# Two attention stages of a two-block transformer: values matmuls of three steps issued together

## The reference, cut to what matters

```python
# stick_breaking_attention, per head
z = einsum('bqhd,bshd->bhqs', q_blk, k) * scale
log_1m = where(causal, log_sigmoid(-z), 0.0)
excl = cumsum(log_1m, axis=3, reverse=True) - log_1m
a = where(causal, exp(log_sigmoid(z) + excl), 0.0)
o = einsum('bhqs,bshd->bqhd', a, v)
# nsa_attention, per kind ("selected" and "window"), per head
s = where(valid, einsum(q_rot, k) * scale, NEG)
o_kind = einsum(softmax(s), v)           # p @ v, twice, plus a compressed branch
out = einsum('bsch,bschd->bshd', gates, [o_cmp, o_sel, o_win]) @ w_o
```

## Time and profile before

| | us |
|---|---|
| median of 3 runs | 2097.75 |
| the profiled execution | 2098.55 |
| its span, first to last instruction | 2096.8 |
| steps of the stick-breaking heads that have an output matmul in them | 902.7 to 1046.9 of the span |
| steps of the NSA heads from the second pair of kinds on | 1571.8 to 1699.5 of the span |

### The profile page before, as it was taken

The page is one execution under the profiler, slowest core; times in us unless marked ns, Lnnn a source line. Parts: engine busy times, 40 slices in busy tenths (PEclk is TensorE's granted clock), DMA queues, the critical chain, the costliest instruction groups (busy, mean ns, idle before and its releaser), DMA issues.

```text
span 2096.8 us, 31979 instructions
## 1 busy us (share of the span) xinstructions
PE 2078.5 (99%) x12566; PEld 1749.0 (83%) x12566; DVE 1520.8 (73%) x2061; ACT 989.0 (47%) x1655; POOL 717.2 (34%) x588
## 2 busy tenths in 40 slices
PE   9999999999999999999999999999999999999998
PEld 6888688888999998777689999988975678899997
DVE  6866775658988886387768787766578757777774
ACT  4433564445544454355554333344537755334344
POOL 2301520027443434054463232301147646323221
PEclk9999999999999999999999999999999999999999
DMA  6233135223323333211133323233520022332321
GB/s 181 91 107 85 51 101 171 71 71 101 106 86 106 116 96 96 81 51 52 40 91 101 121 81 121 83 119 91 152 75 2 1 60 82 101 113 88 115 87 51
DMA packets 293303, 188.44 MB, mean 90 GB/s; under 512 B 9249, under 2 KB 287009, under 8 KB 293153
## 3 DMA queue, kind: packets, MB, share of 16 engines
q1 hardware_dynamic: 292864, 186.18, 29.7%
q10 hardware_dynamic: 288, 0.21, 0.1%
HBM read 183.48 MB, written 2.10 MB: 89 GB/s over the span
## 4 chain that ended last, share of the span: by engine, by line
PE 92%; DVE 4%; ACT 2%; issue 1%; DMA 0%; POOL 0%; ACTq 0%; SPq 0%; DVEq 0%
PE ps L542 90%; PE ps L576 2%; DVE wl L515 1%; ACT wh L505 1%; DVE sb_small L3478 0%; DMA p_xt<-in_x 0%; DVE ns_x L3524 0%; DVE ns_x L3523 0%; DVE tp_up L2330 0%; DVE H L679 0%; DVE nt_pts L3506 0%; DVE st_L L2735 0%; ACT XH L563 0%; DVE tp_up L675 0%; DVE tt_t L2071 0%
## 5 line engine op out<-in xcount | busy, mean ns | idle before, releaser
L515 DVE TENSOR_TENSOR wl<-raw,wh 128x1024 fp32r<-128x1024 f32 (+1 forms) x334 | 429.3, 1299 | 240.5 <-ACT wh L505 239.8
L542 PE MATMUL ps<-xb_x,wh 128*128 128x256 f32 (+1 forms) x1584 | 388.4, 336 | 1.4 <-DVE st_k L2780 0.6
L505 ACT CAST wh<-raw 128x1024 fp32r<-128x1024 f32 (+1 forms) x334 | 322.5, 981 | 132.1 <-PE ps L542 119.9
L542 PEld LDWEIGHTS ps<-xb_x,wh 128*128 128x128 f32 x1584 | 265.6, 188 | 31.1 <-DVE H L679 0.9
L542 PE MATMUL ps<-tt_t,wh 128*128 128x256 f32 x1536 | 277.4, 280 | 0.8 <-ACT tp_q L2257 0.3
L542 PE MATMUL ps<-xb_x,wl 128*128 128x256 f32 (+1 forms) x792 | 264.5, 334 | 0.0
L542 PEld LDWEIGHTS ps<-tt_t,wh 128*128 128x128 f32 x1536 | 237.0, 188 | 5.0 <-ACT tp_q L2257 1.2
L542 PE MATMUL ps<-XH,wh 128*128 128x512 f32 (+1 forms) x616 | 227.5, 369 | 1.2 <-DVE H L709 0.8
L542 PE MATMUL ps<-XH,wl 128*128 128x512 f32 (+1 forms) x616 | 222.5, 361 | 0.0
L542 PE MATMUL ps<-XL,wh 128*128 128x512 f32 (+1 forms) x616 | 222.0, 360 | 0.0
L542 PE MATMUL ps<-tt_t,wl 128*128 128x256 f32 x768 | 214.1, 279 | 0.0
(11 more groups left out here) (442 smaller groups left out, 4552.1 us busy)
## 6 DMA issues: line engine op xcount, KB each, us to landing
raw<-in_mlp_w SPq DMA_DIRECT2D x128, 512.0 KB, 4.0
raw<-in_w_gate_up SPq DMA_DIRECT2D x44, 512.0 KB, 3.9
raw<-in_w_in SPq DMA_DIRECT2D x28, 512.0 KB, 3.7
raw<-in_sb_w_qkv SPq DMA_DIRECT2D x24, 512.0 KB, 3.6
raw<-in_w_down SPq DMA_DIRECT2D x22, 512.0 KB, 5.8
raw<-in_w_out_mix SPq DMA_DIRECT2D x16, 512.0 KB, 3.6
raw<-in_w_kv SPq DMA_DIRECT2D x16, 512.0 KB, 3.8
raw<-in_nsa_w_kv SPq DMA_DIRECT2D x12, 512.0 KB, 3.8
```

The lines of the kernel that those rows point to most:

```text
L505: e.copy(shaped(WH[i % NH], i), source(i)).then_inc(*w_hi.up(i))
L515: e.tensor_tensor(shaped(WL[i % NH], i), source(i), shaped(WH[i % NH], i).bitcast(F), ALU.subtract).then_inc(*w_lo.up(i))
L542: return e.matmul(out, a, b, start=start, stop=stop, skip_group_check=True)
```

## The change

In the stick-breaking stage the outputs of the three steps of a pair are issued one after another at the end of the last of three steps (n % 3 == 2), where before each step issued one. The L buffers become two for each j (six in all, of the width that j needs); `rs1` moves 4096 bytes up. The parts of the q/k projection and of the output projection are dealt out anew over the steps: one k (three matmuls) goes out of the step n % 3 == 2 and one is added in n % 3 == 1; in n % 3 == 0 one k more stands before the cumulative sums and one less behind them. The joint step j = 2 is handled by single heads in ACT, POOL and DVE. In the NSA stage the four values blocks of a group are issued together in the third step, where before they were dealt over three.

```diff
-    rs1 = Phase(PH0 + 92160, "st").sb("rs1", [128, S])
+    rs1 = Phase(PH0 + 96256, "st").sb("rs1", [128, S])
-    Lp = Ring([Buf(ph.sb(f"L{i}", [128, 2, 512])) for i in range(4)])
+    Lp = [Ring([Buf(ph.sb(f"L{j}{i}", [128, 2, wd[j]])) for i in range(2)]) for j in range(3)]
     def parts(n):
-        return [slice(0, 1), slice(1, 2)] if ST[n][1] < 2 else [slice(0, 2)]
+        return [slice(0, 1), slice(1, 2)]
-    QK_BEFORE = {1: (0, 5, 8)}
-    QK_AT = {0: (0, 0, 5), 1: (8, 0, 3), 2: (8, 3, 8)}
-    OUT_AT = {NST - 4: [(0, 0, 2)], NST - 3: [(0, 2, 4)], NST - 2: [(0, 4, 5)], NST - 1: [(0, 5, 6)],
+    QK_BEFORE = {1: (0, 4, 8)}
+    QK_AT = {0: (0, 0, 4), 1: (8, 0, 2), 2: (8, 2, 8)}
+    OUT_AT = {NST - 4: [(0, 0, 1)], NST - 3: [(0, 1, 3)], NST - 2: [(0, 3, 5)], NST - 1: [(0, 5, 6)],
               NST: [(1, 0, 4)], NST + 1: [(0, 6, 7), (1, 4, 7)]}
-            plan(Lp.next(), ("L", n), (mixed, ("so", n)))
+            plan(Lp[j].next(), ("L", n), (mixed, ("so", n)))
...
-            if n >= 3:
-                pe_stick_out(e, n - 3)
+            if n >= 5 and n % 3 == 2:
+                for b in range(n - 5, n - 2):
+                    pe_stick_out(e, b)
...
-    VALUES = {0: (0,), 1: (1,), 2: (2, 3)}
...
-            if n >= 6:
-                for j in VALUES[n % 3]:
+            if n >= 8 and n % 3 == 2:
+                for j in range(4):
                     pe_nsa_values(e, (n // 3 - 2) * 4 + j)
```

## The result

| | before | after |
|---|---|---|
| median of 6 runs, us | 2097.76 (2097.69 to 2097.90) | 2107.05 (2106.45 to 2109.99) |
| ratio after/before | | 1.0047, 95% interval 1.0036 to 1.0057 |
| profiled execution, us | 2098.55 | 2109.99 |
| its span, us | 2096.8 | 2108.2 |

The change makes the kernel 9.3 us slower; 9.2 were forecast. Read by stages in the two profiles: from the first stick-breaking scores to the last matmul of their output projection it took 199.19 us before and takes 194.83 now, 4.4 less; from the first NSA scores to the last values matmul 145.95 before and 162.43 now, 16.5 more. The parts between and behind them are the same within 0.1; the part ahead of them is 0.65 shorter (first stick-breaking scores at 881.64 and 880.99).

A forecast was written before the change was run, and what follows sets the result against it. Both stages were taken to run at TensorE's issue, so shorter lists help unless waits bind. Stick-breaking -3.5 and NSA +12.7 gave +9.2 us, 2107.0 us from a median of 2097.75, range 2098.5 to 2112.5.

The forecast's parts named there:

- Price of a group: TensorE output groups: 0.17 us fixed cost each; four values blocks take 2.31 us joined against 2.62 dealt, saving 0.31.
- Stick-breaking stage: Joined outputs there save 2.3 us, the tail 0.3, a stall 0.9: -3.5 us, bounds -4 to 0.
- The stall at step 24: Stick-breaking step 24: TensorE's wait for DVE's low part before the second head's cumulative sums goes, saving 0.9 us.
- the third rival: Stick-breaking stage loses its 3.5 us gain to DVE's single-head instructions and late q or k: 2110.5 us or more; 15%.
- Third scores: NSA group's third-step scores wait for ACT's exponentials, starting about 4.15 us after the first scores, 0.56 late.
- Turn with a cast: In every second NSA group the third turn's second head waits for DVE's copy: group 9.44 us, +1.37.
- Plain groups: Five NSA groups without extra work: 8.32 us against 8.07, +0.25 each, 1.3 us in all.
- The four mixed groups: NSA groups n = 6, 9, 12, 21, with other DVE work or a stall already: 0.8 us each, 3.2 in all.
- The sum: NSA stage: plain 1.3, pair-output 6.9 and mixed groups 3.2, end 1.3: +12.7 us, bounds 4.8 to 15.
- Full saving: Rival: no wait binds in the NSA stage, so both stages gain, -8.1 us, 2089.6; 10%.
- Only the plain wait: Rival: in NSA groups the exponentials bind everywhere, DVE's copies nowhere: +1.3 us, 2099.1; 12%.
- The stick-breaking stage waiting too: Rival: DVE's single-head instructions and late q or k bring back the 3.5 us: +12.7, 2110.5 or more; 15%.

The follow-up runs named there:

- e3: The whole change, but a group's four values blocks all stand behind the first turn and the cast also waits for the compressed branch: 2091.44 us, ratio 0.9967 to the kernel before.
- e7: Stick-breaking part alone (as e1), with the joint step j = 2 handled as one instruction for both heads: 2094.29 us, ratio 0.9981 to the kernel before.
- e6: Stick-breaking part alone (as e1), with the q/k and output projections dealt as in the kernel before: 2094.32 us, ratio 0.9982 to the kernel before.
- e4: The changed kernel, but ACT's cast and DVE's low part come two steps later, beside the joined values: 2100.23 us, ratio 1.0010 to the kernel before.
- e2: NSA part alone, values joined in the third step, all else as in the kernel before: 2111.32 us, ratio 1.0064.
- e1: Stick-breaking part of the change alone, NSA values dealt over three steps as in the kernel before: 2093.93 us, ratio 0.9979.
- e9: As e3, but joined values behind the second turn and the last-but-one group's values dealt: 2095.38 us, ratio 0.9987 to the kernel before.

## Why the prediction was right, point by point

*Price of a group.* Right: the four values blocks take 2.30 to 2.31 us joined, and e3, which has the joining without the waits, gains in each group.

*Stick-breaking stage: forecast -3.5, measured -4.36.* The joined outputs take 2.31 us:

```profile
912.63 2.38 PE L542 MATMUL ps<-st_L,st_v 128*64 128x256 f32 x20
914.94 0.92 PE L542 MATMUL ps<-st_q,st_k 64*128 64x256 f32 x8
```

The stall at step 24 is gone. Mis-sized was the edit that I costed at nothing, the single heads in the joint step. The stage before had a second stall, which the prediction did not name:

```profile
892.52 0.73 PE L542 MATMUL ps<-xb_x,wh 128*128 128x512 f32 x2 [0.55 <-DVE st_k L2780]
```

By e7 the single heads take it away (0.8) and cost 0.4 in two pairs, where k is now late. The other half of the difference is not settled. That nothing else becomes late was right but for these 0.4 us, the third rival in small; that the new deal was needed was not: by e6 it is worth 0.4 us.

*Third scores: forecast 4.15, measured 4.15* in 13 of 14 groups; the pattern read before any values matmul was the pattern of all.

*Turn with a cast: forecast a group of 9.44, measured 9.43.* e4 shows the cause by moving the cast. Plain groups: 8.32 forecast, 8.32 measured in one; 8.66 in another (n = 27), in which the second head's turn starts at 1642.02, 0.15 us after POOL's scaling of it ended; that chain was left out of the sum. The four mixed groups came to 3.5 us, 3.2 forecast, by a middle value that no row had priced; the end came to 1.3, as forecast.

*The sum: forecast +12.7 for NSA*, +13.2 in e2's profile. The profile of the change has +16.5, and 3.3 of these are the two falls of the clock, which the prediction did not name. That the median of the runs, 2107.05, fell on the forecast is owed in part to two errors that cancel: the stick-breaking stage gave 0.9 more than forecast, the NSA stage took that much more: 0.5 by the waits, as e2 shows, and the rest perhaps by falls of the clock. How many falls the unprofiled runs had is open.

*The rule on PSUM* of the Trainium skill (TensorEngine Tiling (Array Packing), PSUM Bottleneck), that a TensorE made quicker by tiling does not quicken the emptying of PSUM, agrees with the runs: the copy of head 1 ended at 6.60 before and after. Of the rule on mode changes (same page, Key Properties) the runs show a fixed cost for each group, 2.31 us joined against 2.62 dealt, and not the draining that it names.

*Rivals.* Full saving: refuted for this change, though e3, which removes the waits, comes within 2 us of its 2089.6. Only the plain wait: refuted by the waits for L3506. The stick-breaking stage waiting too: refuted by e1, which gained 4.3 us.

## What to carry to other kernels

Before work is moved on the engine that is the bound, ask of each wait on its list how far it is from binding and how much of that distance is the work being moved: here 1.25 us of slack before the third scores and 0.3 before the turn, against 1.8 us taken out. A stretch of the same loop where that work is still absent (the first group) shows what it covers. Then put the joined work where the slack is needed. The whole kernel is 6.8 us faster with the values behind the first turn (e3), 2.8 faster behind the second (e9) and 9.3 slower behind the third. The stick-breaking part gives 4.3 us of each, so the join of the values itself brings 2.5 us in the first place and costs 1.5 in the second (where one group stays dealt) and 13.6 in the third.

## What the runs showed of the hardware that was not expected

A wait of 0.89 us, at the end of 6.62 us in which TensorE was busy 5.33, was followed by a stretch at the lower clock in two groups of six with such a wait in one execution, and in none of e2's profile, whose waits are the same; each fall cost 1.64 us. In e4's profile a fall of 1.65 us followed waits of 0.88 and 0.41 us, which stand in the kernel after too, without a fall. So where a fall follows, such a wait has cost nearly three times its length (0.89 + 1.64 us), and this is not so in every run. What sets off a fall in one execution and not in another is open.
